# Adding expert rows onto the residual stream: loads and VectorE additions, or accumulating transfers

## The reference, cut to what matters

```
h = h + mixer(rmsnorm(h))
h = h + hierarchical_moe(rmsnorm(h))        # out[token] += w0 * y(expert 0) + w1 * y(expert 1)
if layer == 0:
    k_nope, k_rope, v = shared_latent_kv(h)  # for layer 1's attention
...
return rmsnorm(h, final_norm)[:, 16:]
```

## Time and profile before

| | |
|---|---|
| median of 3 runs | 2077.43 us (2074.22 to 2080.18) |
| the profiled execution | 2074.01 us, its span 2072.1 us |
| busy share: PE, DVE, ACT, POOL | 93%, 39%, 25%, 9% |
| mean granted TensorE clock | 0.964 |
| DMA traffic | 307.83 MB, mean 149 GB/s |
| stage after layer 0's experts | from 1077.8 us to 1218 us of the span |
| last stage | from 2031.3 us to the end |

### The profile page before, as it was taken

The page is one execution under the profiler, slowest core; times in us unless marked ns, Lnnn a source line. Parts: engine busy times, 40 slices in busy tenths (PEclk is TensorE's granted clock), DMA queues, the critical chain, the costliest instruction groups (busy, mean ns, idle before and its releaser), DMA issues. The chain is left out here.

```text
span 2072.1 us, 30279 instructions
## 1 busy us (share of the span) xinstructions
PE 1929.0 (93%) x12117; PEld 1090.9 (53%) x12117; DVE 797.9 (39%) x1877; ACT 521.2 (25%) x1262; POOL 196.1 (9%) x289
## 2 busy tenths in 40 slices
PE   9999999788997998999988999999999997999990
PEld 4545554578643884334435657677665555333330
DVE  0105667766353454121115524434343216121215
ACT  0003333433111330111133433333332111111112
POOL 0000002001162211111100000000000000111100
PEclk9999999899998989999999999999999997999995
DMA  4200100020022327999965000000023015899976
GB/s 143 81 26 1 41 21 4 1 84 4 2 93 72 144 104 278 400 412 422 423 270 198 8 1 1 1 1 1 1 82 136 31 41 216 349 413 422 422 325 270
DMA packets 47077, 307.83 MB, mean 149 GB/s; under 512 B 9248, under 2 KB 9568, under 8 KB 26944
## 3 DMA queue, kind: packets, MB, share of 16 engines
q1 hardware_dynamic: 33824, 267.48, 32.1%
q0 software_dynamic: 13104, 38.29, 4.7%
HBM read 282.34 MB, written 35.72 MB: 153 GB/s over the span
## 5 line engine op out<-in xcount | busy, mean ns | idle before, releaser
L253 PE MATMUL psum<-arena 64*64 64x64 f32 (+12 forms) x10850 | 1796.4, 408 | 88.8 <-issue 23.5
L253 PEld LDWEIGHTS psum<-arena 128*128 128x128 f32 (+4 forms) x10850 | 956.6, 158 | 878.4 <-issue 770.2
L2274 DVE TENSOR_TENSOR arena<-psum,arena 128x256 f32<-128x256 f32 x44 | 18.7, 425 | 370.9 <-ACT arena L2326 362.2
L1567 ACT ACTIVATE arena<-arena 128x1024 f32<-128x1024 f32 x43 | 45.4, 1056 | 244.1 <-DVE arena L3025 105.6
L2939 ACT ACTIVATE arena<-psum,arena 128x1024 f32<-128x1024 f32 (+8 forms) x72 | 50.2, 699 | 188.7 <-DVE arena L2975 188.7
L2364 POOL DMA_INDIRECT arena<-xn_rows,arena x44 | 44.8, 1017 | 460.6 <-PE psum L2239 243.7
L2326 ACT ACTIVATE arena<-psum 128x256 f32<-128x256 f32 x44 | 17.0, 385 | 280.6 <-PE psum L253 280.6
L1267 ACT ACTIVATE arena<-psum 128x256 f32<-128x256 f32 (+3 forms) x128 | 43.9, 355 | 106.7 <-PE psum L253 95.7
L2317 ACT ACTIVATE arena<-psum,arena 128x512 f32<-128x512 f32 x44 | 30.3, 688 | 141.9 <-PE psum L253 141.9
L2369 POOL DMA_INDIRECT expert_rows<-arena x44 | 44.1, 1003 | 216.1 <-ACT arena L2317 190.3
L2968 DVE TENSOR_TENSOR psum<-psum,arena 128x128 f32<-128x128 f32 (+2 forms) x72 | 20.4, 283 | 103.4 <-PE psum L253 103.1
(11 more groups left out here) (307 smaller groups left out, 1267.5 us busy)
## 6 DMA issues: line engine op xcount, KB each, us to landing
arena<-in_w_exp SPq DMA_DIRECT2D x64, 2048.0 KB, 16.8
arena<-in_w_exp SPq DMA_DIRECT2D x64, 1024.0 KB, 18.6
arena<-expert_rows SPq DMA_DIRECT2D x16, 1024.0 KB, 7.3
xn_rows<-arena SPq DMA_DIRECT2D x16, 512.0 KB, 2.6
arena<-in_w_out SPq DMA_DIRECT2D x8, 512.0 KB, 7.8
arena<-in_x SPq DMA_DIRECT2D x8, 512.0 KB, 3.5
arena<-in_w_o SPq DMA_DIRECT2D x1, 4096.0 KB, 13.4
out<-arena SPq DMA_DIRECT2D x8, 512.0 KB, 3.7
```

Source lines behind the costliest of these rows:

```text
L253: return e.matmul(out, lhsT, rhs, start=start, stop=stop, skip_group_check=True)
L1567: return e.activation(junk, h[:, s, :], ACT.Square, accum_out=sq_sum[:, s:s + 1])
```

## The change

In layer 0 SP loads only the first row of each token (512 KB a tile, `sp_first_row`), into one of four buffers instead of two. The second row is added onto h by a transfer that POOL issues with `accum_op=ALU.add` (`pool_add`): source in DRAM, destination h's tile in SBUF. VectorE waits for both and adds the first row (`dve_first_row`). POOL issues its nine accumulating transfers ahead of the loads of `w_uq`, `w_uv` and `w_uk`, and the wait for two loads that stood there is gone. Five semaphores, those of the gathers and scatters (`d_xe + d_y`), are used in turn, and from the sixth transfer on POOL waits for the one that was issued five before.

In the last stage the first four tiles are treated in the same way. For the other four both rows are added by accumulating transfers, twelve in all, in the order of `ADDS`: the first row of a tile is issued two tiles behind its second row, and after that has landed. VectorE has nothing to add for these four; ScalarE's square waits for the transfer. `fin_row` gets its place in a weight buffer of layer 1 that is free after block 18, and SP issues its load behind the last weight load of that layer.

```
@@ in build, after sp_over and the other overflow helpers
-        def dve_combine(e, y, s, c, m_c):
+        d_add = d_xe + d_y
+        def pool_add(e, i, s, j, m_add):
             n = SLOT[s][1]
+            if i >= len(d_add):
+                e.wait_ge(*m_add[i - len(d_add)])
+            e.dma_start(h[0:n, s, :], y_pairs[P * s:P * s + n, D * j:D * (j + 1)], accum_op=ALU.add).then_inc(d_add[i % len(d_add)].sem, 16)
+        def sp_first_row(e, s, c, sem):
+            n = SLOT[s][1]
+            e.dma_start(c[0:n, :], y_pairs[P * s:P * s + n, 0:D]).then_inc(sem.sem, 16)
+        def dve_first_row(e, y, s, c, m_c, m_a):
+            n = SLOT[s][1]
+            e.wait_ge(*m_a)
             e.wait_ge(*m_c)
-            for j in range(2):
-                if j:
-                    e.wait_ge(*y.h_out.last())
-                e.tensor_tensor(h[0:n, s, :], h[0:n, s, :], c[0:n, j, :], ALU.add).then_inc(*y.h_out.up())
-        def sp_combine(e, s, c, sem):
-            n = SLOT[s][1]
-            e.dma_start(c[0:n].rearrange("p a b -> p (a b)"), y_pairs[P * s:P * s + n, :]).then_inc(sem.sem, 16)
+            e.tensor_tensor(h[0:n, s, :], h[0:n, s, :], c[0:n, :], ALU.add).then_inc(*y.h_out.up())
@@ def sp_latent
-                if s >= 2:
-                    e.wait_ge(*layers[0].h_out.at(2 * (s - 2) + 2))
-                sp_combine(e, s, c_lat[s % 2], d_c[s % 2])
+                if s >= 4:
+                    e.wait_ge(*layers[0].h_out.at(s - 3))
+                sp_first_row(e, s, c_lat[s % 4], d_c[s % 4])
@@ def sp_experts
+                elif b == GU_FREED + 1:
+                    e.wait_ge(*y.ex.full(("gu", GU_FREED)))
+                    e.dma_start(fin_row, io["rows"][5:6, :].to_broadcast([P, D])).then_inc(d_fin.sem, 16)
@@ def pool_latent
-            for s in range(2):
-                e.wait_ge(*m_cl[s])
+            for s in range(NS):
+                pool_add(e, s, s, 1, m_al)
             e.dma_start(w_uq, io["w_uq"]).then_inc(d_lu.sem, 16)
...
@@ the last stage
+        N_FIN = 4
+        ADDS = [(s, 1) for s in range(N_FIN)]
+        for s in range(N_FIN, NT + 2):
+            ADDS += [(s, 1)] * (s < NT) + [(s - 2, 0)] * (s - 2 >= N_FIN)
...
+        def pool_final(e):
+            for i, (s, j) in enumerate(ADDS):
+                if j == 0:
+                    e.wait_ge(*m_of[s, 1])
+                pool_add(e, i, s, j, m_add)
         def dve_final(e):
             for d, s in turns(NT, 3):
-                if d == 0:
-                    dve_combine(e, layers[1], s, c_fin[s % 4], m_cf[s])
+                if d == 0 and s < N_FIN:
+                    dve_first_row(e, layers[1], s, c_fin[s], m_cf[s], m_of[s, 1])
@@ def act_final
-                    e.wait_ge(*layers[1].h_out.at(2 * s + 2))
+                    e.wait_ge(*(layers[1].h_out.at(s + 1) if s < N_FIN else m_of[s, 0]))
@@ def sp_final
-            e.dma_start(fin_row, io["rows"][5:6, :].to_broadcast([P, D])).then_inc(d_fin.sem, 16)
-            for s in range(4):
-                sp_combine(e, s, c_fin[s], d_c[s])
+            for s in range(N_FIN):
+                sp_first_row(e, s, c_fin[s], d_c[s])
             for s in range(NT):
-                if s + 4 < NT:
-                    e.wait_ge(*layers[1].h_out.at(2 * s + 2))
-                    sp_combine(e, s + 4, c_fin[s], d_c[s])
                 e.wait_ge(*fin_rows.at(s + 1))
```

More of the change, by code:

```diff
@@ L92 @@
 GU_TOP, DN_TOP = 5, 1
+GU_FREED = max(USED[_n][-1] for _n in range(NE) if GU_IN[_n] == GU_TOP)
 FREED = max([USED[_n][-1] for _n in range(NE) if GU_IN[_n] == GU_TOP] + [USED[_n][-1] for _n in range(NE) if DN_IN[_n] == DN_TOP])
@@ L2556, in build @@
         lat_junk = take(D)
-        c_lat = [take(2, D) for _ in range(2)]
+        c_lat = [take(D) for _ in range(4)]
         assert top[0] <= base_top
-        m_cl = [d_c[s % 2].nth() for s in range(NS)]
+        m_cl = [d_c[s % 4].nth() for s in range(NS)]
+        m_al = [d_add[s % len(d_add)].nth() for s in range(NS)]
         LAT = 9
@@ L2640, in act_latent @@
                 if d == 0:
-                    e.wait_ge(*layers[0].h_out.at(2 * s + 2))
+                    e.wait_ge(*layers[0].h_out.at(s + 1))
                     if s:
@@ L2709, in dve_latent @@
                 if d == 0:
-                    dve_combine(e, layers[0], s, c_lat[s % 2], m_cl[s])
+                    dve_first_row(e, layers[0], s, c_lat[s % 4], m_cl[s], m_al[s])
                 elif d == 1:
@@ L2997, in build @@
         plan_layer(1)
-        layers[1].h_out = layers[0].h_out.after(2 * NS)
+        layers[1].h_out = layers[0].h_out.after(NS)
         top[0] = base_mla - D
@@ L3100, in build @@
         top[0] = base_b2
-        fin_junk, fin_row = take(D), take(D)
-        c_fin = [take(2, D) for _ in range(4)]
+        fin_row = arena[:, layers[1].gu_at[GU_TOP]:layers[1].gu_at[GU_TOP] + D]
+        fin_junk = take(D)
+        N_FIN = 4
+        c_fin = [take(D) for _ in range(N_FIN)]
         assert top[0] <= base_top
         o_fin = [take(D) for _ in range(3)]
-        m_cf = [d_c[s % 4].nth() for s in range(NT)]
+        m_cf = [d_c[s].nth() for s in range(N_FIN)]
+        ADDS = [(s, 1) for s in range(N_FIN)]
+        for s in range(N_FIN, NT + 2):
+            ADDS += [(s, 1)] * (s < NT) + [(s - 2, 0)] * (s - 2 >= N_FIN)
+        m_add = [d_add[i % len(d_add)].nth() for i in range(len(ADDS))]
+        m_of = {key: m for key, m in zip(ADDS, m_add)}
         d_out = d_xs
@@ L3199, in _ @@
             pool_moe(e, layers[1])
+            pool_final(e)
         @block.sync
```

## The result

The changed kernel took 2096.06 us in the median of five runs (2088.33 to 2099.11), beside 2077.43 for the kernel before on the same chip: ratio 1.008, 95% interval [1.0066, 1.0095], so 14 to 20 us slower. The forecast was 2070.2 us, faster; the time lies above the range's upper end of 2090.

What follows compares the result with a forecast made beforehand. VectorE and the DMA engines were taken to bound the last stage, TensorE's idle lead-in the other gain. Terms -5.6 and -1.6 gave -7.2 us: 2066.8 for the profiled execution, 2070.2 against the median; range 2063 to 2090.

Steps and rivals of the forecast that it cites:

- The bound of the last stage: Last stage: VectorE full from 2038 on, DMA engines full from 2034 to 2058 at 391 to 423 GB/s.
- Price of an accumulating transfer: Both stages: 512 KB added by a transfer cost 1.25 us, as a plain load; upper end 2.5 us.
- every accumulation reads twice: Both stages: h's old rows are read too, 2.5 us a transfer; in all +11.2, 2088.6 us; chance 0.32.
- Transfer-bound before and after: Both stages: engines full anyway, price between, 1.9 us a piece; +1.9, 2079.3 us, no change; chance 0.25.
- chain of landings: Last stage, tiles with both rows accumulated: one transfer waits for another, last row 3.9 us later, sum -3.3; no separate chance.
- the mark of being wrong altogether: Last stage: squares of tiles 4 to 7 coming more than 3.8 us apart would refute the prediction.
- Sharing the engines evenly: Layer 0's lead-in: SP and POOL share the engines, POOL's first 512 KB need 2.5 us, landing 0.9 us later than now.
- POOL's issue: Both stages: issuing one accumulating transfer occupies POOL for 1 us, bounded by 0.59 and twice that.
- The transfer floor: Last stage: 16 rows (20.0 us), five stores (6.25) and 1.1 to landing from 2033; end 5.6 us earlier.
- the early load of the gain: Last stage: fin_row loaded behind layer 1's last weight load costs nothing and removes 1.25 us of traffic.
- w_uq behind nine accumulations: After layer 0: weight loads queued later on POOL cost nothing, 12 us in hand, about 1 us at 2.5 a piece.
- TensorE's clock: Layer 0's lead-in: shorter idle time might spare the low clock and return some 2 us; none counted.

## Why the prediction was wrong, point by point

**The bound of the last stage** was read rightly: VectorE full, and the DMA engines full beside it. The consequence was drawn too mildly. In a stage where the engines have no time left, relieving VectorE can bring little, and an unknown price of engine work decides whether it turns into a loss.

**The step that failed** is "Price of an accumulating transfer: I take 1.25 us". It measured 2.48 to 2.58 alone and 2.65 in place. Twelve at 1.40 us more than I took are 16.8 us; the forecast of -5.6 would then be +11.2, and the stage became 10.7 us longer. That these lie so close is partly luck: by the runs the stage gained 2.2 us with plain transfers, and accumulating cost 12.9 on top. I chose the lower end because plain loads were the nearest rows, while the upper end had an argument from the trace: stores were charged like loads, so a read of the old rows would be too. The Trainium skill, Collectives: The Full Stack, section on the bandwidth ceiling and the fold count, gives 1.93 for the add of a reduce-scatter against the plain copy of an all-gather, both between cores; this case's 1.9, for loads of one core, alone and in place, agrees with it. Which second pass the engines make no run shows; that the time nearly doubles is shown. A second read of the source in DRAM it is not, as far as the page's line on HBM counts: 282.34 MB read before and after, and 294.92 with the 24 transfers behind the end, which is one read of 512 KB for each, accumulating or plain. That leaves the read of h's old rows in SBUF as the likely one, not shown.

**The rival "every accumulation reads twice"** had the mechanism, the sign and most of the last stage (+9.4 against +10.7), on the same floor for plain transfers that proved too low. In layer 0 it had +1.8 against +3.65 in this pair of profiles and some 3 by the medians. "Transfer-bound before and after" and its chain of landings fall: the share has no gap while the accumulations run, and the price is not in between. The squares of tiles 4 to 7 came 5.8, 3.4 and 3.0 us apart, the first gap over the 3.8 that I had named as the mark of being wrong altogether. In that gap two accumulations landed, at 2074.7 the one that POOL waited for ahead of its last issue and at 2076.9 tile 5's, so twice 2.65 us of the engines' time account for most of it.

**"Sharing the engines evenly"** is the second step that failed, and the one that took the gain of layer 0. I let the first accumulation land 0.9 us later than the old load; by the same count at the doubled price 3.3 us later. It was 6.0 in layer 0 and 4.8 in the last stage. There it came as if behind all of SP's four rows; for layer 0, where the same code scatters by over 3 us, that is not shown. What I counted behind it held: 2.5 us saved in the lead-in by additions against 2.3 measured.

**POOL's issue** was taken at 1 us and measured 0.92 (4.60 for five), within the bounds, and POOL's stream began 1.05 and 1.17 us after SP's, as taken. Neither moved the sum.

**The transfer floor** was too low in itself. With plain transfers the last square came 32.5 us after SP's issue (2064.97 against 2032.51), where I had 29.1, and the stage gained 2.2 us, not 5.6. As the early load alone gave 1.7, the twelve additions that VectorE was spared brought about 0.5, hardly more than the 0.4 between two profiles of the old stage (40.8 and 41.2). For 8 us the engines moved less than 420 GB/s (windows of the run with plain transfers):

```profile
2050.00:2054.00 4.00, 0.00 (x0) 0.00 (x0) 3.04 (x5) 1.45 (x3) 0.66 (x2) 0.50 0.94 301
2054.00:2058.00 4.00, 0.00 (x0) 0.00 (x0) 1.16 (x2) 1.44 (x3) 0.00 (x0) 0.50 1.00 354
```

Near there POOL waited 7.5 us for a landing before its last issue at 2058.43. How much of the gap to 29.1 us these waits make was not tried. In layer 0 the lead-in with plain transfers took 15.9 us against 14.48, 1.4 longer and not 1.6 shorter, though within the 14.0 to 17.0 of the old code. So even with the price that I took, the two stages would have come to about -0.8 us, no change: the price decided between no change and slower, and the gain itself wasn't there.

**Costed at nothing and rightly so:** the early load of the gain (the run with it alone), and w_uq behind nine accumulations. Its cover shrank as predicted for the doubled price and was enough: w_uv, the later of the two loads that VectorE wants there, landed 21.6 us after its issue at 1103.44, so at 1125.0, and L2710 began at 1125.89. **TensorE's clock** in the lead-in stayed low, after TensorE had stood idle from 1086.1:

```profile
1088.00:1092.00 4.00, 0.00 (x0) 0.00 (x0) 0.70 (x1) 0.00 (x0) 0.44 (x1) 0.52 1.05 273
1092.00:1096.00 4.00, 0.93 (x5) 0.93 (x6) 2.32 (x4) 1.44 (x3) 1.04 (x2) 0.50 1.06 249
```

That is the lower of its two levels, 1.2 of 2.4 GHz, in these windows of the kernel after, and the first transposes took 1.97 us where they took 1.56 before. The gain that I had named and not counted didn't come.

## What to carry to other kernels

An addition moved into a transfer is paid in DMA time: here 512 KB cost 2.5 to 2.65 us instead of 1.3 to 1.4, so look first for a stage where the engines have time left, and the windows' share beside their GB/s tells that before any edit. Where the price of a new operation stands in no row and the sign hangs on it, a few lines behind the kernel's end that time it alone are worth more than an argument. Where two bounds lie close together (VectorE full and the DMA engines full in the same windows), relieving one is worth little: here plain transfers gave 2.2 us of a stage of 40.8, and 1.7 of these came from the early load of the gain. And before a few microseconds of one stage are explained, the same code's stage should be read in several profiles: here the last stage repeated within 0.4 us, the lead-in only within 3.

## What the runs showed of the hardware that I had not expected

- In the last stage POOL's first transfer lands as late as if it waited for all of SP's rows, though it was issued 1.2 us after the first of them: 10.5 us with four rows ahead, 8.1 with two, 5.4 alone. A plain one does likewise (issued at 2033.67, used at 2042.32: 8.7 us against 3.9 to 4.1 alone); where it was issued only 0.2 us after SP's first row, in the run with all transfers plain, it took 7.0.
- An accumulating direct transfer occupies POOL longer at its issue than a plain one, 0.85 us against 0.55 when alone. The plain weight loads right behind the accumulations of layer 0 took 0.80 to 0.84 us too (0.53 to 0.59 in the kernel before), which no run here explains.
- GpSimd's and VectorE's additions slow each other: 3.01 us against 1.22 for VectorE, and 2.9 (8.58 for three) against 2.0 for GpSimd's first one. The Trainium skill, SBUF — State Buffer, section on who interferes with whom, says that a VectorE instruction with two inputs in SBUF contends with a GpSimd instruction that reads SBUF; these rows agree.
